# A delta-rule inverse whose X is the transposed, updated transpose, copied by ScalarE; exponentials and weight remainders behind it; a weave of its own for the first pair

## The reference, cut to what matters

```python
gc = jnp.cumsum(g, axis=-1)
decay = jnp.exp(jnp.where(causal, gc[..., :, None] - gc[..., None, :], -jnp.inf))
k_beta = k * beta[..., None]
a_low = jnp.where(strict, jnp.einsum("bhnid,bhnjd->bhnij", k_beta, k) * decay, 0.0)
t_mat = a_low + jnp.eye(L, dtype=f32)
rhs = jnp.concatenate([v * beta[..., None], k_beta * jnp.exp(gc)[..., None]], axis=-1)
sol = lax.linalg.triangular_solve(t_mat, rhs, left_side=True, lower=True, unit_diagonal=True)
u = sol[..., :dv]
w = sol[..., dv:]
attn = jnp.where(causal, jnp.einsum("bhnid,bhnjd->bhnij", q, k) * decay, 0.0)
...
v_new = u_i - jnp.einsum("bhld,bhde->bhle", w_i, state)
o = (jnp.einsum("bhld,bhde->bhle", q_i * jnp.exp(g_i)[..., None], state)
     + jnp.einsum("bhlm,bhme->bhle", a_i, v_new))
```

## Time and profile before

| | us |
|---|---|
| median of three runs | 906.73 (905.78 to 906.95) |
| the profiled execution, its own time | 907.24 |
| its span in the trace | 905.4 |
| TensorE busy | 883.1 (98%) |
| TensorE weight loads busy | 818.7 (90%) |
| VectorE busy | 587.7 (65%) |
| ScalarE busy | 524.7 (58%) |
| mean granted clock of TensorE | 0.992 |

### The profile page before, as it was taken

The page is one execution under the profiler, slowest core; times in us unless marked ns, Lnnn a source line. Parts: engine busy times, 40 slices in busy tenths (PEclk is TensorE's granted clock), DMA queues, the critical chain, the costliest instruction groups (busy, mean ns, idle before and its releaser), DMA issues. The chain is left out here.

```text
span 905.4 us, 17940 instructions
## 1 busy us (share of the span) xinstructions
PE 883.1 (98%) x7098; PEld 818.7 (90%) x7098; DVE 587.7 (65%) x955; ACT 524.7 (58%) x924; POOL 24.6 (3%) x36
## 2 busy tenths in 40 slices
PE   8999999999999999999999898999999999999998
PEld 6988899999998999999989898989988999999986
DVE  4589765555556576669776868555758555545576
ACT  6478744444446856566757485846458444444463
POOL 4100300000000000000000000000000000000000
PEclk8999999999999999999999999999999999999999
DMA  9814765555553455454314141424556565566541
GB/s 281 271 53 133 170 191 187 187 188 188 191 191 120 144 184 185 143 162 138 116 57 132 48 140 48 150 85 157 178 194 208 163 199 192 171 202 197 174 162 47
DMA packets 107655, 143.24 MB, mean 158 GB/s; under 512 B 3032, under 2 KB 95448, under 8 KB 107600
## 3 DMA queue, kind: packets, MB, share of 16 engines
q1 hardware_dynamic: 105648, 137.60, 47.0%
q0 software_dynamic: 1744, 4.67, 2.3%
q10 hardware_dynamic: 208, 0.20, 0.1%
HBM read 141.41 MB, written 1.05 MB: 157 GB/s over the span
## 5 line engine op out<-in xcount | busy, mean ns | idle before, releaser
L1201 DVE TENSOR_TENSOR wl<-w_raw,wh 128x1024 fp32r<-128x1024 f32 x251 | 305.2, 1224 | 225.6 <-ACT wh L637 225.0
L1824 PE MATMUL ps<-xTh,wh 128*128 128x256 f32 (+1 forms) x1160 | 330.8, 285 | 0.9 <-DVE xTl L1227 0.8
L1826 PE MATMUL ps<-xTh,wl 128*128 128x256 f32 (+1 forms) x1160 | 326.3, 281 | 0.0
L1825 PE MATMUL ps<-xTl,wh 128*128 128x256 f32 (+1 forms) x1160 | 326.3, 281 | 0.0
L637 ACT ACTIVATE wh<-w_raw 128x1024 fp32r<-128x1024 f32 x251 | 263.4, 1054 | 81.1 <-PE ps L1832 60.1
L1824 PEld LDWEIGHTS ps<-xTh,wh 128*128 128x128 f32 x1160 | 219.0, 189 | 4.6 <-issue 2.7
L1825 PEld LDWEIGHTS ps<-xTl,wh 128*128 128x128 f32 x1160 | 218.3, 188 | 1.9 <-issue 1.0
L1826 PEld LDWEIGHTS ps<-xTh,wl 128*128 128x128 f32 x1160 | 219.3, 189 | 0.0
L1830 PE MATMUL ps<-wh,y 128*128 128x512 f32 x224 | 87.9, 392 | 0.0
L1832 PE MATMUL ps<-wh,y 128*128 128x512 f32 x224 | 87.6, 391 | 0.0
L1831 PE MATMUL ps<-wl,y 128*128 128x512 f32 x224 | 87.1, 389 | 0.0
(11 more groups left out here) (382 smaller groups left out, 1279.3 us busy)
## 6 DMA issues: line engine op xcount, KB each, us to landing
w_raw<-in_w_in_dram SPq DMA_DIRECT2D x42, 1024.0 KB, 5.2
w_raw<-in_w_ff_dram SPq DMA_DIRECT2D x32, 1024.0 KB, 5.3
w_raw<-in_w_ffn_gate_dram SPq DMA_DIRECT2D x11, 1024.0 KB, 5.3
w_raw<-in_w_ffn_up_dram SPq DMA_DIRECT2D x11, 1024.0 KB, 5.3
w_raw<-in_w_ffn_down_dram SPq DMA_DIRECT2D x11, 1024.0 KB, 4.9
w_raw<-in_w_out_dram SPq DMA_DIRECT2D x8, 1024.0 KB, 5.0
w_raw<-in_w_proj_a_dram SPq DMA_DIRECT2D x4, 1024.0 KB, 5.2
w_raw<-in_w_proj_b_dram SPq DMA_DIRECT2D x4, 1024.0 KB, 5.2
```

What stands on the lines that cost most here:

```text
L1201: TT(low_part, raw_unit(SLOT[p], j, layout), high_part.bitcast(F32), ALU.subtract).then_inc(w_lo, 1)
L1824: mm(out, wh_, xh, start=first, stop=False)
L1825: mm(out, wh_, xl, start=False, stop=False)
L1826: return mm(out, wl_, xh, start=False, stop=last)
```

## The change

It has four parts.

1. **The inverse.** VectorE no longer updates `Xc`. TensorE transposes the updated `XTc` (`x_rows`, a product with the identity, in the place of `x_times`), now behind `times_a` of the same group, and ScalarE copies the even half-blocks of that into `Xc` (`x_level`). The copies of `XT_` stay on ScalarE, behind the five levels.
2. **The decays.** `eg` stays ahead of the inverse on ScalarE, with a semaphore of its own (`eg_out`), on which those who only need bank `mb` or the order now wait. The eight exponentials go behind `u0` in stage 6, in pairs 0 to 2. Ahead of the first pair's own stages both are done as before.
3. **The remainders.** VectorE does none after stage 4 and two after stage 6.
4. **The first pair's weave.** `GDN_FIRST` has 13 steps after stage 1 and 15 after stage 3, where `GDN_WEAVE` has 9 and 19.

```diff
+GDN_FIRST = [2, 13, 8, 15, 10, 2, 4, 3, 3, 4]
...
                         first_taps(a)
-                        decays(a + 1)
+                        decay_columns(a + 1)
+                    for lv in range(1, 6):
+                        x_level(lv, a)
                     for g in range(2):
                         act.wait_ge(lv_xt[g], a * 6 + 5)
                     act.activation(XT_[0:HB, :, 0:HB], XTc[0:HB, :, :], ACT.Copy)
-                    act.activation(XT_[HB:P, :, HB:P], XTc[HB:P, :, :], ACT.Copy).then_inc(xt_full, 1)
+                    act.activation(XT_[HB:P, :, HB:P], XTc[HB:P, :, :], ACT.Copy).then_inc(lv_x[1], 1)
                 if s == 6:
                     act.wait_ge(uw_ps, a + 1)
                     act.activation(u0, acc[:, 3, 0:256].rearrange("p (j n) -> p j n", j=2), ACT.Copy).then_inc(u0_out, 1)
+                    if not final:
+                        decays(a + 1)
...
+            def decay_columns(b):
+
+                act.wait_ge(t12_out, b + 1)
+                act.activation(eg, mb[:, 256:512].rearrange("p (j n) -> p j n", j=2), ACT.Exp).then_inc(eg_out, 1)
+
             def decays(b):
 
-                act.wait_ge(t12_out, b + 1)
-                act.activation(eg, mb[:, 256:512].rearrange("p (j n) -> p j n", j=2), ACT.Exp)
...
+            def x_level(lv, a):
+
+                for g in range(2):
+                    act.wait_ge(lv_zx[g], a * 5 + lv)
+                    act.activation(half_blocks(Xc[:, 2 * g:2 * g + 2, :], lv, 0), half_blocks(pairs(fm[:, g, 0:P]), lv, 0),
+                                   ACT.Copy).then_inc(lv_x[g], 1)
...
                         for g in range(2):
-                            dve.wait_ge(lv_zx[g], a * 5 + lv)
-                            grow(Xc[:, 2 * g:2 * g + 2, :], lv, 0, half_blocks(pairs(fm[:, g, 0:P]), lv, 0)).then_inc(lv_x[g], 1)
                             masked(g, lv + 1, a)
...
-                    n = {4: 1, 5: 0, 6: 1, 7: 1, 8: 0}.get(s, 8) if weave is GDN_WEAVE else 8
+                    n = {4: 0, 5: 0, 6: 2, 7: 1, 8: 0}.get(s, 8) if weave is not MOBA_WEAVE else 8
...
-            def x_times(g, a):
+            def x_rows(g):
 
                 for j in range(2):
                     pr, out = 2 * g + j, fm[:, g, j * HB:(j + 1) * HB]
                     for part in blocks:
-                        last = mm(out[part], PM_[part, pr, :], Xc[part, pr, :], start=True, stop=True)
+                        last = mm(out[part], XTc[part, pr, :], ident[part, part], start=True, stop=True)
                 last.then_inc(lv_zx[g], 1)
...
                     for g in range(2):
+                        times_a(g, lv + 1, a)
                         if lv == 1:
                             bank_ready(g, 2 * P_GDN + 14 + g, 8, a)
-                        x_times(g, a)
-                        times_a(g, lv + 1, a)
+                        x_rows(g)
```

## The result

| | us |
|---|---|
| before, in the comparison with the changed kernel | 905.89 (904.78 to 906.95, 8 runs) |
| after | 908.32 (906.75 to 908.78, 8 runs) |
| ratio | 1.0024, 95% interval 1.0014 to 1.0035 |
| profiled execution after, its own time | 908.22 |
| its span | 906.4 |

The kernel became slower by about 0.24%. The forecast was 906.4 and "the same"; the time lies inside its range, but the sign was missed.

The account below looks back on a forecast made before the run. TensorE works almost the whole span, so edits pay only where it waits or runs at half clock. Terms sum to +0.9 us, or -0.3 with one clock drop gone; from the median 906.73 this gives 906.4 us, range 903.4 to 909.4.

Parts of the forecast that it names:

- remainders: Ahead of the inverses of pairs 0 to 2: VectorE's copies start 1.13 us earlier, -3.4 us in all.
- behind the first level, four inverses: Later four levels of each inverse: 1.73 us instead of 1.77, -0.6 us in all.
- first level, pairs 1 and 2: First level of these inverses: 0.12 us longer than the former 1.61 us, +0.25 us in both.
- late ScalarE, pair 0: First level, pair 0: ScalarE, behind a table load and eg, copies X late, +1.0 us.
- late ScalarE, pair 3: First level, pair 3: ScalarE is still in the 2048-column sigmoid, so the second level starts late, +1.4 us.
- decays: Behind the inverse, pairs 0 to 2: exponentials between u0 and S1 delay v_new by 0.75 us each, +2.25 us.
- from an eviction's end to the next product 0.05 us: Link in each inverse level: a 0.05 us gap, read from rows of before, taken also behind ScalarE's new copy.
- one stretch left of two: Clock in the inverses: one of two half-clock stretches goes, -1.2 us.
- rival A: The clock stays up in all four inverses: 905.2 us; chance 0.22.
- B: Inverse levels: ScalarE's copy hides its latency, the masked copy sets levels of 1.55 to 1.61 us: 903.7 us; chance 0.10.
- C: First-level waits for ScalarE in pairs 0 and 3 drop the clock, three or four stretches: 908.9 or 910.1 us; chance 0.17.
- D: Behind the inverse: v_new is not delayed, because TensorE arrives later or S1 is not held: 904.2 us; chance 0.06.

Follow-up runs that it names:

- e7: Changed kernel with the pair 3 sigmoid on ScalarE moved from stage 5 to stage 9, behind the output: 906.92 us, ratio 1.0007.
- e1: Kernel before with only the new table of remainders (none after stage 4, two after stage 6): 901.16 us, ratio 0.9946.
- e10: Kernel before with only the first pair's own weave: 905.7 us, ratio 0.9999.
- e6: Changed kernel with TensorE's two waits swapped, for the copy of X first and then the masked copy: 906.61 us, ratio 1.0007.
- e13: e1 with TensorE's two waits swapped, for X first and then the masked copy, which ends last there: 902.65 us, ratio 0.9964.
- e2: Changed kernel with the eight exponentials moved from behind u0 to between ScalarE's copies of X of levels 1 to 4: 905.71 us, ratio 0.9998.
- e9: Changed kernel with the old table of remainders put back: median 913.22 us, ratio 1.0085.
- e8: Changed kernel with ScalarE's weight half of stage 7 done behind the copy of v_new: 907.41 us, ratio 1.001.
- e14: e1 with ScalarE's weight half of stage 7 also put behind the copy of v_new, as in e8: 899.50 us, ratio 0.9928.
- e3: Kernel before with the new remainders and the transposing inverse, but VectorE copying X behind its masked copy; decays stay beside the inverse: 904.17 us, ratio 0.9979.
- e4: Changed kernel with ScalarE copying all 128 columns of X instead of the 64 new ones: 909.49 us, ratio 1.0038.

## Why the prediction was wrong, step by step

First a base that can be compared. The profiled execution of the kernel before, 907.24, has two half-clock stretches in its inverses, and the profiled one after, 908.22, has none. Pair 0's costs 1.21 us by the prediction's own rows (10.57 and not 9.36). Pair 1's costs 1.29, since that inverse lasts from 501.94 to 512.59, 10.65 us:

```profile
501.94 0.68 PE L2204 MATMUL ps<-R 64*64 64x64 f32 x16 [0.24 <-DVE R L1638]
...
512.59 0.39 PE L1830 MATMUL ps<-wh,xTh 128*128 128x256 f32 x1
```

Together with the offset of 0.36 us ahead of the rounds, the change costs 0.98 + 0.36 + 2.50 = +3.8 us at unchanged clock, where my sum was +0.9.

The times of the kernel before, over all comparisons of this case, form three groups: 904.0 to 904.8 (7 times), 905.2 to 906.1 (50) and 906.7 to 907.3 (31). It is tempting to take them as no, one and two stretches. The mean granted clocks do not bear this out by themselves: the lowest group has 0.996 in each of its six runs that have a recorded clock, the middle one 0.998. Of these two groups no trace was read. A half-clock stretch can also lie where it costs little: the profiled execution of before has a third one at 8 to 16 us (granted clock 0.57), and is only 0.3 us behind after there. Nor is this peculiar to before: one run of after is 906.75 at 0.998, where the others are 908.22 to 908.78 at 0.999 or 1.0, and two runs of e7 are 905.6 at 0.997, where the others are 906.7 to 907.5. What sets the groups stays open.

| term | predicted | measured | from |
|---|---|---|---|
| remainders | -3.4 | -3.4 | waits 5.9 to 2.5; 3.5 in the trace of e1 |
| behind the first level, four inverses | -0.6 | +1.5 | three levels of 1.87 and not 1.77, the fourth 1.70 and not 1.66, the way out 0.05 to 0.13 longer |
| first level, pairs 1 and 2 | +0.25 | +0.5 | 1.87 and not 1.61 |
| late ScalarE, pair 0 | +1.0 | +1.1 | first level 456.48 - 453.77 = 2.71 |
| late ScalarE, pair 3 | +1.4 | +1.5 | first level 593.76 - 590.70 = 3.06 |
| decays | +2.25 | +2.7 | 0.88, 0.88, 0.89 a round from `u0` to v_new |
| first pair's weave | 0 | 0 | e10 |
| sum | +0.9 | +3.9 | +3.8 by the traces as a whole |

The two late first levels, each with the wait in brackets:

```profile
453.77 0.68 PE L2220 MATMUL ps<-R 64*64 64x64 f32 x16 [0.24 <-DVE R L1654]
...
456.48 0.33 PE L2220 MATMUL ps<-R 64*64 64x64 f32 x4 [0.80 <-ACT R L1058]
```

```profile
590.70 0.68 PE L2220 MATMUL ps<-R 64*64 64x64 f32 x16 [0.24 <-DVE R L1654]
...
593.76 0.45 PE L2220 MATMUL ps<-R 64*64 64x64 f32 x8 [1.15 <-ACT R L1058]
```

**Right.** The gain of the remainders, the two late copies and their sizes, the delay of v_new, the wait that only moves in the first pair: all at the named places. That ScalarE's copy, and not the masked one, would be ready last before each level was right too, and its record of 0.23 us is the 0.22 taken. The Trainium skill (ScalarE: Activation LUTs, "What ACT_TABLE_LOAD costs") gave an estimate of 0.24 for it, and the trace agrees with 0.23; neither says anything of the link behind it.

**The step that failed: "from an eviction's end to the next product 0.05 us", carried over to the new chain.** My level was 1.71 to 1.75 us and is 1.87. Two links were too short. The larger one, 0.09 us, is the gap behind ScalarE's copy: 0.14 and not 0.05. The rows of before did show 0.05, but for a wait that stands first of two. In the change the wait that ends last stands second. e6 and e13 show this from both sides: swapping the waits takes 0.09 off where it is X that is late, and adds as much where it is the masked copy. It is worth the 1.5 us of e6. The smaller one, 0.05 us, is from the product with A to the transposing product, 0.28 (459.11 to 459.39) where I had 0.23: so it is for the first group, which starts behind a wait, and only the second group's products follow each other in 0.23 to 0.24. Why was not tested. Together the two terms of the levels came out 2.4 us too small, most of the missing 3.0. A misreading that hardly counts stands beside it: I gave four later levels 1.77 us in each inverse, where the last one is 1.66 before.

**The size of the decays.** 0.9 us a round and not 0.75, another 0.4 us. The exponentials start 0.41 behind u0's start (466.49 to 466.90), where I let 0.28 pass; they last 2.36 us for eight, as taken. S1 starts at 469.26, and v_new follows 3.16 us later (472.42), as before:

```profile
466.49 0.39 ACT L1018 ACTIVATE R<-ps 128x256 f32<-128x256 f32 x1 [1.66 <-PE ps L2303]
466.90 0.40 ACT L1050 ACTIVATE R<-R 128x128 f32<-128x128 f32 x1
...
469.26 0.36 ACT L1023 ACTIVATE R<-ps 128x256 f32<-128x256 f32 x1
...
472.42 0.37 ACT L1030 ACTIVATE R<-ps 128x256 f32<-128x256 f32 x1
```

That none of it is hidden is what e2 shows: -2.6 us.

**The clock.** I had one stretch left of two. The stretches went, as rival A had it, although TensorE waits 1.15 us in pair 3's first level. Stretches came back where the wait ahead of an inverse was 1.9 us (e9) and once at 1.1 us (e8). The rule of the Trainium skill (TensorE: Matmul & The Clock Gate, "What's actually happening"), that recent activity keeps the gate open, agrees with the direction of this. It does not tell which wait is followed by a stretch: behind three waits of 1.8 to 1.9 us before and e10 have two stretches and e9 one; behind two waits of 1.1 us e8 has one and e14 none.

The account closes on the profiled executions. My sum gave 906.9 there and 908.22 was measured, 1.3 more: +3.0 from the terms, -1.3 from the second stretch that also went, -0.4 from the offset ahead of the rounds. That the forecast of 906.4 is off by 1.9 comes on top from its base: the median of three runs lay 0.5 below the profiled execution before, and the median after 0.1 above the one after. The second stretch and a start that happened to be earlier hid 1.7 of the 3.0 us. Without them the time would be near 910, outside my range; that it lies inside is luck.

**Rivals.** B (ScalarE's latency hidden, levels of 1.55) is out, since the copy is last in every level. C (more stretches) and D (v_new not late) are out. Slower came by a mechanism that I had given no case of its own: the chain of a level simply longer than taken. My bounds for the copy alone (0.16 to 0.38) would have allowed it: with 0.38 in place of 0.22 the level is 1.89. I had kept that end for the record's length, and gave the long end no chance.

**What stays open.** Why a late wait in second place costs 0.09 us more; the runs show that it does, on two operands and behind two engines. Why the first group's two products are 0.28 us apart. What sets the three groups of times, and the offset that executions have ahead of the rounds.

## What to carry to other kernels

Before trading operations between engines on a latency chain, draw the new chain link by link, and take each link from a row with the same conditions: which wait ends last, in which place, behind what. Where TensorE waits for two things, put the wait that ends last first. When a wait is taken away, ask which other chain runs beside it: in e8 ScalarE's chain into the next round kept most of the gain. And change an order by one piece at a time: here one remainder moved was worth more than the whole change around it, and the next one of the same kind ran into the weights of its own round.

## What the runs showed of the hardware that was not expected

- Two waits of TensorE in a row: from the end of the copy that is ready last to the product 0.05 us if its wait stands first, 0.14 to 0.15 if it stands second (e6 and e13 against after and e1). In 16 to 18 levels this is 1.5 to 1.7 us of run time.
- The copy of 128x64 from PSUM takes the same 0.23 us on ScalarE and on VectorE (e3), 0.28 for 128x128 on ScalarE (e4).
- Shorter waits are no sure gain at the clock: e8 took away 3.3 us of waits behind the inverse, and one inverse fell to the 1.2 GHz level after a wait of 1.1 us that had been 0.8. It is no rule either: with the same waits of 1.1 us e14 kept 2.4 GHz in all of them.
- A half-clock stretch in an inverse does not always cost the same: 1.2 to 1.3 us in before, e8 and e10, 0.8 us in e9.
